# Layer norm statistics of a decoder layer: from ScalarE squares to VectorE batch norm statistics

## What is computed

```python
def layer_norm(x, g, b):
    xf = x.astype(jnp.float32)
    mu = jnp.mean(xf, axis=-1, keepdims=True)
    var = jnp.mean(jnp.square(xf - mu), axis=-1, keepdims=True)
    return ((xf - mu) * lax.rsqrt(var + LN_EPS) * g + b).astype(x.dtype)
...
for l in range(DEPTH):
    h = hybrid_mixer(x, ...)
    x = layer_norm(ALPHA * x + h, ln1_g[l], ln1_b[l])
    h = memory_cross_attention(x, mem, w_xq[l], w_xkv[l], w_xo[l])
    x = layer_norm(ALPHA * x + h, ln2_g[l], ln2_b[l])
    h = swiglu(x, w_ffn_in[l], w_ffn_out[l])
    x = layer_norm(ALPHA * x + h, ln3_g[l], ln3_b[l])
```

## Time and profile before

| | |
|---|---|
| time, median of 3 runs | 923.52 us (923.49 to 925.54) |
| profiled execution, span | 922.0 us |
| TensorE matmul busy | 889.6 us (96%) |
| VectorE busy | 438.2 us (48%) |
| ScalarE busy | 297.7 us (32%) |
| GpSimd busy | 69.8 us (8%) |
| chain that ended last | PE 87%, VectorE 5%, ScalarE 4%, issue 2%, DMA 1%, POOL 1% |
| `squares` (L964) | 12 x 1.15 us, from 467.1 to 915.8 us |
| `var` (L783) on GpSimd | 12 x 0.19 to 1.29 us |
| `rstd` (L786) on GpSimd | 12 x 0.55 to 1.60 us |

### The profile page before, as it was taken

One profiled execution on the slowest core, in us unless ns is written; L12 is line 12 of the kernel. 1 busy time (PEld: TensorE's weight loads), 2 busy tenths in 40 slices (PEclk: granted clock), 3 DMA queues, 4 the chain that ended last, 5 costly groups with the idle time before them and its releaser, 6 DMA issues.

```text
span 922.0 us, 11603 instructions
## 1 busy us (share of the span) xinstructions
PE 889.6 (96%) x4511; PEld 735.3 (80%) x4511; DVE 438.2 (48%) x833; ACT 297.7 (32%) x552; POOL 69.8 (8%) x103
## 2 busy tenths in 40 slices
PE   7999999988989999999999889999999999999996
PEld 7988897776558888888889769888888888888885
DVE  3244346679752525252766775344433333322344
ACT  3112156137743222222323643222222222221221
POOL 2100000162420000000011010000000000000001
PEclk9999999999999999999999899999999999999998
DMA  7524521420002322225532211222233323222321
GB/s 263 157 91 117 135 92 32 130 92 2 1 1 72 107 96 92 91 91 205 199 98 83 101 46 47 92 91 91 91 94 112 111 92 136 91 92 92 99 107 68
DMA packets 70007, 89.89 MB, mean 97 GB/s; under 512 B 2685, under 2 KB 61895, under 8 KB 69967
## 3 DMA queue, kind: packets, MB, share of 16 engines
q1 hardware_dynamic: 69583, 88.92, 29.7%
q0 software_dynamic: 384, 0.43, 0.3%
HBM read 86.81 MB, written 2.52 MB: 97 GB/s over the span
## 4 chain that ended last, share of the span: by engine, by line
PE 87%; DVE 5%; ACT 4%; issue 2%; DMA 1%; POOL 1%; SPq 0%; DVEq 0%; POOLq 0%; ACTq 0%
PE ps L1572 26%; PE ps L1573 26%; PE ps L1574 26%; ACT prob L820 2%; PE ps L1750 2%; PE ps L1724 1%; PE ps L1699 1%; DMA x_nat<-in_x 1%; DVE prob L1184 1%; DVE w_lo L1061 1%; PE ps L1609 1%; PE ps L2023 1%; DVE prob L1163 1%; PE ps L2024 1%; PE ps L2025 1%
## 5 line engine op out<-in xcount | busy, mean ns | idle before, releaser
L1572 PE MATMUL ps<-xt_hi,w_hi 128*128 128x512 f32 (+1 forms) x712 | 274.6, 386 | 4.5 <-DVE xt_lo L1067 2.1
L1573 PE MATMUL ps<-xt_hi,w_lo 128*128 128x512 f32 (+1 forms) x712 | 273.7, 384 | 0.0
L1574 PE MATMUL ps<-xt_lo,w_hi 128*128 128x512 f32 (+1 forms) x712 | 273.7, 384 | 0.0
L1572 PEld LDWEIGHTS ps<-xt_hi,w_hi 128*128 128x128 f32 x712 | 133.8, 188 | 32.7 <-DVE w_lo L1061 2.4
L1574 PEld LDWEIGHTS ps<-xt_lo,w_hi 128*128 128x128 f32 x712 | 133.8, 188 | 26.6
L1573 PEld LDWEIGHTS ps<-xt_hi,w_lo 128*128 128x128 f32 x712 | 133.8, 188 | 26.3
L798 ACT CAST w_hi<-raw 128x1024 fp32r<-128x1024 f32 (+1 forms) x59 | 60.9, 1036 | 188.6 <-PE ps L1574 172.6
L1061 DVE TENSOR_TENSOR w_lo<-raw,w_hi 128x1024 fp32r<-128x1024 f32 (+1 forms) x59 | 71.2, 1210 | 100.6 <-ACT w_hi L798 97.7
L1528 DVE TENSOR_TENSOR w_lo<-raw,w_hi 128x1024 fp32r<-128x1024 f32 x40 | 48.9, 1222 | 79.1 <-ACT w_hi L1020 79.1
L1349 DVE TENSOR_TENSOR w_lo<-raw,w_hi 128x1024 fp32r<-128x1024 f32 x30 | 36.7, 1223 | 91.5 <-ACT w_hi L946 91.5
L1020 ACT CAST w_hi<-raw 128x1024 fp32r<-128x1024 f32 x40 | 41.9, 1047 | 78.8 <-PE ps L1574 78.8
(11 more groups left out here) (246 smaller groups left out, 1315.6 us busy)
## 6 DMA issues: line engine op xcount, KB each, us to landing
raw<-in_w_in SPq DMA_DIRECT2D x25, 1024.0 KB, 5.0
raw<-in_w_ffn_in SPq DMA_DIRECT2D x22, 1024.0 KB, 4.9
raw<-in_w_ffn_out SPq DMA_DIRECT2D x11, 1024.0 KB, 4.8
raw<-in_w_mix_out SPq DMA_DIRECT2D x4, 1024.0 KB, 4.9
x_nat<-in_x SPq DMA_DIRECT2D x4, 512.0 KB, 4.9
raw<-in_w_branch_b SPq DMA_DIRECT2D x4, 512.0 KB, 3.9
resid<-in_x SPq DMA_DIRECT2D x1, 2048.0 KB, 9.7
raw<-in_w_xkv SPq DMA_DIRECT2D x2, 1024.0 KB, 6.0
```

Source lines behind the costliest of these rows:

```text
L1572: pe.matmul(dst, a_hi, b_hi, start=start, stop=False)
L1573: pe.matmul(dst, a_lo, b_hi, start=False, stop=False)
L1574: return pe.matmul(dst, a_hi, b_lo, start=False, stop=stop)
```

## The change

VectorE makes the statistics itself: after each half's residual add (now without the written-out sum) it waits for that half and runs `bn_stats` on it (six numbers per row), after both halves `bn_aggr` (mean and variance), and adds the epsilon. ScalarE's `square` and the buffer it wrote are gone. GpSimd only raises to -0.5. The norm's first step takes the mean instead of its negative. Padding keeps the other tiles where they were.

```diff
-        row_sum = sb("row_sum", [P, TT, 2])
-        neg_mean = sb("neg_mean", [P, TT])
-        sq_sum = sb("sq_sum", [P, TT])
+        half_stats = sb("half_stats", [P, TT, 2, 6])
+        mean_var = sb("mean_var", [P, TT, 2])
...
-            squares = sb("squares", [P, D], BF16, keep)
+            sb("pad_gb", [P, 512], F32, keep)
...
             for n in range(3 * TT):
                 t = n % TT
-                pool.wait_ge(sq_done, n + 1)
-                pool.tensor_scalar(var[:, t:t + 1], sq_sum[:, t:t + 1], 1.0 / D, LN_EPS, ALU.mult, ALU.add).then_inc(pool_step, 1)
-                steps += 1
-                pool.wait_ge(pool_step, steps)
+                pool.wait_ge(var_done, n + 1)
                 pool.tensor_tensor(rstd[:, t:t + 1], var[:, t:t + 1], half[:, 0:1], ALU.pow).then_inc(rstd_done, 1)
...
-            def square(n):
-                t = n % TT
-                act.wait_ge(mean_done, n + 1)
-                if n:
-                    act.wait_ge(sq_done, n)
-                act.activation(squares[:, :], resid[:, t, :], ACT.Square, bias=neg_mean[:, t:t + 1],
-                               accum_out=sq_sum[:, t:t + 1]).then_inc(sq_done, 1)
...
                     v = resid[:, t, c * 512:(c + 1) * 512]
-                    dve.scalar_tensor_tensor(out=v, in0=v, scalar=ALPHA, in1=ps[:, 2 * t + c, :], op0=ALU.mult, op1=ALU.add,
-                                             accum_out=row_sum[:, t, c:c + 1]).then_inc(y_done, 1)
-                dve.wait_ge(y_done, 2 * n + 2)
-                dve.tensor_scalar(neg_mean[:, t:t + 1], row_sum[:, t, 0:1], row_sum[:, t, 1:2], -1.0 / D, ALU.add,
-                                  ALU.mult).then_inc(mean_done, 1)
+                    dve.scalar_tensor_tensor(out=v, in0=v, scalar=ALPHA, in1=ps[:, 2 * t + c, :], op0=ALU.mult,
+                                             op1=ALU.add).then_inc(y_done, 1)
+                    dve.wait_ge(y_done, 2 * n + c + 1)
+                    link(dve.bn_stats(half_stats[:, t, c, :], v))
+                link(dve.bn_aggr(mean_var[:, t, :], half_stats[:, t, :, :].rearrange("p c x -> p (c x)")))
+                dve.tensor_scalar(var[:, t:t + 1], mean_var[:, t, 1:2], LN_EPS, None, ALU.add).then_inc(var_done, 1)
...
-                dve.wait_ge(sq_done, n + 1)
-                link(dve.scalar_tensor_tensor(out=v, in0=v, scalar=neg_mean[:, t:t + 1], in1=gb[:, 0, :], op0=ALU.add, op1=ALU.mult))
+                link(dve.scalar_tensor_tensor(out=v, in0=v, scalar=mean_var[:, t, 0:1], in1=gb[:, 0, :], op0=ALU.subtract, op1=ALU.mult))
                 dve.wait_ge(rstd_done, n + 1)
```

More of the change, by code:

```diff
@@ L72 @@
 LINE_PAD = 112
+PAD_LINE = 104
 N_TAB_A = 3 * (P // ROW_COPIES)
@@ L347, in build_layer @@
         half = sb("half", [P, 1])
-        sb("pad_line", [P, 8 + 128])
+        sb("pad_line", [P, PAD_LINE])
         with ExitStack() as st:
@@ L449, in build_layer @@
         merge_step, ffn_step = sem("merge_step"), sem("ffn_step")
-        rows_done, y_done, mean_done, sq_done, rstd_done, norm_done, gb_in = (
-            sem("rows_done"), sem("y_done"), sem("mean_done"), sem("sq_done"), sem("rstd_done"), sem("norm_done"), sem("gb_in"))
+        rows_done, y_done, var_done, rstd_done, norm_done, gb_in = (
+            sem("rows_done"), sem("y_done"), sem("var_done"), sem("rstd_done"), sem("norm_done"), sem("gb_in"))
         memkv_out, xq_ps, xq_out, zero_ready = sem("memkv_out"), sem("xq_ps"), sem("xq_out"), sem("zero_ready")
@@ L970, in turn_tile @@
                     turn_drain(2 * t + hf, 2 * TT * k + 2 * t + hf)
-            square(0)
-            square(1)
             turn_tile(1, 0)
-            square(2)
             turn_tile(1, 1)
-            square(3)
             turn_tile(1, 2)
@@ L999, in _ @@
                         pt_drain(nn)
-            square(TT)
-            square(TT + 1)
             turn_tile(2, 0)
             turn_tile(2, 1)
-            square(TT + 2)
             split(PF + 2)
             split(PF + 3)
-            square(TT + 3)
             turn_tile(2, 2)
@@ L1039, in _ @@
                 split(PO + n)
-            for t in range(TT):
-                square(2 * TT + t)
         @block.vector
@@ L1414, in norm_last @@
                 link(dve.scalar_tensor_tensor(out=sa[:, :, :].rearrange("p a c -> p (a c)"), in0=resid[:, t, :],
-                                              scalar=neg_mean[:, t:t + 1], in1=gb[:, 0, :], op0=ALU.add, op1=ALU.mult))
-                dve.wait_ge(sq_done, n + 1)
+                                              scalar=mean_var[:, t, 0:1], in1=gb[:, 0, :], op0=ALU.subtract, op1=ALU.mult))
                 dve.wait_ge(rstd_done, n + 1)
@@ L1563, in _ @@
                 else:
-                    dve.wait_ge(mean_done, 3 * TT)
                     norm_last(2 * TT + t)
```

## The result

The changed kernel takes 928.43 us (median of 10 runs, 926.83 to 930.03), the kernel before 923.72 us in the same comparison (10 runs, 921.79 to 925.54). The ratio of their runs is 1.0042, with a 95% interval of 1.0029 to 1.0054: slower by 2.7 to 5.0 us. The profiled execution of the change spans 925.6 us against 922.0.

What follows compares the result with a forecast made beforehand. The prediction took VectorE's in-order queue in norm 2 as the bound. Norm 2 +4.2, norm 1 -0.3, norm 3 +0.3 and clock +0.7 gave +4.9 us on the median 923.52: 928.4 us, range 925.2 to 931.5.

Steps and rivals of the forecast that it cites:

- What bounds the kernel: Norm 2, 541 to 552 us: VectorE's in-order queue is the bound, busy 9.75 of 11 us.
- Prices: VectorE's steps per tile: bn_stats 0.70 us, bn_aggr 0.19, sums 3.25 against 1.45, so 1.80 us more.
- Waits cost VectorE time: On VectorE, a step behind a waited-for add starts after 0.72 us instead of 0.60: 0.12 us per wait.
- Norm 2 step by step: Norm 2: TensorE's waits grow to 2.63 and 3.5 us, a new one of 1.06 appears; 4.2 us lost.
- Norm 3, last tile: End of kernel: VectorE waits for GpSimd's power, first store-ready half comes 0.3 us later.
- Norm 1: Norm 1's last tile: TensorE's 0.32 us wait at 498 goes, a gain of 0.3 us.
- Clock: After norm 2's longer TensorE waits the granted clock falls for a short time, costing 0.7 us.
- The round trip: Norm 2: the chain through ScalarE and GpSimd was the bound, so the change is faster, 921.0 us; chance 0.05.

Runs made afterwards that it cites:

- Experiments 1: Changed kernel with ScalarE's squares put back in norm 2, new statistics in norms 1 and 3 only: 924.14 us, ratio to the kernel before 0.9995.
- experiment 2: Kernel before with the new statistics in norm 2 alone: 928.70 us, ratio to the kernel before 1.0041.
- experiment 6: Changed kernel with each of norm 2's eight bn_stats done twice: 935.03 us (4 runs), ratio to the kernel before 1.0119.
- experiment 7: Changed kernel with bn_stats done twice for tiles 0 to 2 of norms 1 and 3: 926.91 us, ratio to the kernel before 1.0034.
- experiment 5: Changed kernel with both adds ahead of the statistics in norm 2 and idle matmuls in TensorE's two waits there: 926.69 us, ratio to before 1.0033.
- the filled pair: Kernel before and changed kernel, both with idle matmuls in TensorE's long waits (cross-attention and norm 2): 922.15 and 925.77 us.
- experiment 3: Changed kernel with 8 and 11 idle matmuls in TensorE's two waits in norm 2: 927.55 us, ratio to the kernel before 1.0037.
- experiments 7 and 4: experiment 7, and the changed kernel with both adds ahead of the statistics in norm 2, waits unfilled: the latter 926.77 us, ratio to before 1.0016.
- filled changed kernel: Changed kernel with idle matmuls in all three long waits (8 in the cross-attention, 8 and 11 in norm 2): 925.77 us, ratio to before 1.0013.

## Why the prediction was right

The prediction said 928.4 us, slower; it is 928.43. Step by step, by its own terms:

- **What bounds the kernel** (VectorE's queue in norm 2): right. Experiments 1 and 2 put the whole loss there, experiment 6 shows that the queue passes on every microsecond (5.82 of 5.8), experiment 7 that norm 3 passes on none and norm 1 0.39 us of some 4.4.
- **Prices**: bn_stats 0.69 us where I took 0.70, bn_aggr 0.21 (0.19), a tile's sums 3.21 (3.25). The 512-wide, one-value-per-step reading of the rows held, and both ends (0.43 and 1.28) fell. The Trainium skill's 58 cycles and one per element, the page "VectorE: DVE Perf Modes", section "The TRN2 errata — SBUF-src ops pay a fixed extra latency per instruction", would have made it 0.59 us: 0.10 too short here. The same section says itself that this row comes out too low against a measured fixed part of about 150 cycles, and gives 691 ns for a float32 add of 512; the trace's 694 ns agree with that.
- **Waits cost VectorE time**: right. Next to the changed kernel, experiment 5 leaves away three waits between neighbours per tile and is 1.18 us shorter in norm 2, some 0.10 us for each. The Trainium skill's rule in the same page, section "Rules for kernel authors", that the drain follows every op regardless and semaphores need not be spared, does not hold in these rows.
- **Norm 2 step by step**, from its first add: tile 0's transposes after 9.99 us predicted, 9.98 measured; first feed-forward matmul 18.16 and 18.09; tile 2's transposes 25.07 and 24.94, with a wait of 1.06 predicted and 0.83 measured. The sum of 4.2 came out as 4.21. The wait before the first feed-forward matmul was forecast at 3.5 us; it was 1.81, because the clock had fallen ahead of it, and 3.39 in experiment 7, where it had not.
- **Norm 3, last tile**: +0.3, measured +0.28, with the wait for GpSimd of 0.52 us that was forecast.
- **Norm 1**: right in sign, too small: 0.3 forecast, 0.54 in the profile of the change and in the filled pair. I took the row's idle time of 0.32 us as the whole price of TensorE's wait. In the stream around it matmuls start 0.12 us apart; over the wait, two starts lie 0.60 apart (497.81 to 498.41 in the kernel before). The wait costs the distance of the starts less the usual distance, 0.48, since the idle time is counted from the end of a matmul that is 0.28 long and would have been overlapped; the next start comes 0.07 late as well (498.41 to 498.60), and together that is the 0.54.
- **Clock**: this term failed for the profiled execution. I expected a fall behind the longer waits, and it came (0.66 from 546 to 551), but I priced it at 0.7 us on the path. It costs nothing there (experiment 3, 382.11 against 382.10): the slow rows of tile 3 fill idle time. My working looked for the price behind the second wait only and not at what the clock does between the two. The case that I did price, a full second wait with the fall behind it, is that of experiments 7 and 4: it cost 0.42 us in the one (382.52 against 382.10) and 0.81 in the other (381.73 against 380.92).
- **The round trip** (the faster rival): falls; it had read the chain's 3.94 us on ScalarE and GpSimd as removable, while VectorE's queue stood behind it with 0.51 us to spare. The idle time that I gave VectorE for the earlier statistics, 0.69 us, was too small: the timeline has 0.46 us before 539.04 and 0.33 before 540.25 besides, 1.48 in all. That is still short of the 2.5 us that the rival needed.

By the profile the terms give -0.54 + 4.21 + 0.28 = 3.95 us, and the ratio of the runs says 3.9; the medians say 4.7. So the forecast's 4.9 was a little high, by the clock's 0.7 us and norm 1's 0.24, and that its time fits the median to 0.1 us is in part luck. Whether norm 2's clock costs the changed kernel anything in a part of its runs stays open. Two of its ten runs (929.17 and 930.03 us, the slowest) have a mean granted clock of 0.987 where the other eight have 0.989, but the mean doesn't say where in the kernel the clock fell. The filled changed kernel's median stands 2.7 us under the unfilled one's of another comparison (925.77, 928.43), which is hardly more than the 2.4 us that filling gave the kernel before in its own.

## What to carry to other kernels

Taking a round trip over two other engines out of a chain gains nothing where the engine that takes over the work is the one whose queue bounds the stretch: count what it has to do between the two events, and its idle time, before reading the chain. Place such an edit by stage: the same statistics were free between norm 3's long matmuls, a gain of half a microsecond at the end of norm 1, where the latency counted, and a loss of 1.05 us per tile where the queue was full. Where TensorE must wait 2 us or more, a few idle matmuls in the wait can be worth more than the edit (here 2.4 us), and they can take away spread that hides small gains: the runs of the kernel before lie within 6.9 us (29 runs) without and 2.8 us (12 runs) with the filling, though those of the filled changed kernel still within 4.5.

## What was not expected of the hardware

- The same wait of TensorE lowers the clock in some executions and not in others. After the wait of 2.25 us before the cross-attention's last transposes the granted clock was 0.51 to 0.57 from 524 to 531 us in nine profiles and 1.00 in one; after the wait of 2.12 us in norm 2 it stayed 1.00 in two and averaged 0.57 over four us in a third; after the wait of 2.62 us before tile 0's transposes it fell in the profiles of the change and of experiment 2 (0.66 and 0.72 from 546 to 551) and not in that of experiment 7. No run here shows what decides it. It was worth 1.5 to 1.9 us each time where TensorE set the pace, 0.4 to 0.8 where a wait for VectorE stood behind it and took up a part, and nothing where that wait took up all. It makes some of the 4 to 7 us between the fastest and slowest runs of the kernel before (921.6 to 928.4): their mean granted clock is 0.992 to 0.994 in the fastest and 0.986 in the slowest run of each of the three comparisons. In experiment 2 one run of twelve took 924.23 us at a mean clock of 0.994, the other eleven 927.78 to 930.20 at 0.988 to 0.990.
- GpSimd's 128x1 power takes 0.55 us alone and 1.52 next to a 1.28 us step of VectorE with two inputs in SBUF; next to the same step cut in halves it took 0.98.
